# Values products of two query tiles at a time in the dense halves of two attention mixers

## The reference

```python
# first mixer, dense: every query sees all 512 keys
s = (q_nope @ k_nope + q_rope @ k_rope) * scale
o_a = softmax(s) @ v
# first mixer, banded: keys at a distance of at most 128
o_b, lse = banded_attention(qb, kb, vb, 128, 128)
o_b = o_b * sigmoid(lse - sink)
# second mixer: three dilated branches, joined by the softmax of their log sums;
# and attention to a neighbourhood of 8 rows by 16 columns of a 64-column grid, with a bias
o_c = dilated_attention(rope(q_c), rope(k_c), v_c)
o_d = neighborhood_attention(q_d, k_d, v_d, rpb)
```

## Time and profile before

| | |
|---|---|
| median of 3 runs | 2587.31 us |
| profiled execution | 2588.96 us, its span 2586.9 us |
| TensorE (PE) busy | 2502.2 us, 97% |
| DVE, POOL, ACT busy | 1447.5, 723.4 and 553.5 us |
| mean granted clock of TensorE | 0.986 of full speed |
| attention, first mixer | about 132 to 241 us and 349 to 448 us |
| attention, second mixer | about 1383 to 1527 us and 1630 to 1800 us |

### The profile page before, as it was taken

How to read it: one execution, slowest core, us unless ns; L and a number is a source line. 1 busy time by engine, 2 the same in 40 slices (tenths; PEclk the granted TensorE clock), 3 DMA queues, 4 the chain that set the end, 5 groups by cost and what they waited for, 6 DMA issues and landing times. The chain is left out here.

```text
span 2586.9 us, 37035 instructions
## 1 busy us (share of the span) xinstructions
PE 2502.2 (97%) x13964; PEld 1383.0 (53%) x13964; DVE 1447.5 (56%) x2210; ACT 553.5 (21%) x1400; POOL 723.4 (28%) x799
## 2 busy tenths in 40 slices
PE   8999999999999999999899999999989999999997
PEld 4456556445555555555344554454446555565563
DVE  2465456347766866765135332443257767767764
ACT  2164145111111111111103330332111111111112
POOL 2286358123112112120005430542032122121111
PEclk9999999999999999999899999999989999999998
DMA  7100030337999999997600122014249999999986
GB/s 199 27 9 14 1 147 18 116 147 293 330 355 347 341 356 337 345 354 263 214 28 17 54 62 89 17 46 160 98 175 338 345 353 337 345 355 335 354 325 228
DMA packets 177342, 534.91 MB, mean 207 GB/s; under 512 B 32464, under 2 KB 47312, under 8 KB 177232
## 3 DMA queue, kind: packets, MB, share of 16 engines
q1 hardware_dynamic: 166432, 499.34, 51.7%
q0 software_dynamic: 10800, 34.09, 5.8%
HBM read 490.39 MB, written 44.56 MB: 207 GB/s over the span
## 5 line engine op out<-in xcount | busy, mean ns | idle before, releaser
L1857 PE MATMUL bank<-ring,arena 128*64 128x256 f32 x4096 | 479.8, 382 | 2.1 <-DVE arena L2132 1.7
L1868 PE MATMUL bank<-ring,arena 128*128 128x512 f32 x1024 | 453.8, 602 | 1.8 <-ACT arena L1956 1.8
L917 PE MATMUL bank<-ring,arena 128*128 128x512 f32 (+1 forms) x1024 | 430.2, 576 | 1.7 <-issue 0.8
L1857 PEld LDWEIGHTS bank<-ring,arena 128*64 128x64 f32 x4096 | 291.7, 137 | 168.1 <-issue 30.2
L1570 POOL TENSOR_SCALAR arena<-arena 128x512 f32<-128x512 f32 (+2 forms) x256 | 328.0, 1298 | 183.8 <-DVE arena L1446 175.8
L1857 PE MATMUL bank<-arena 128*64 128x256 f32 x3072 | 364.4, 379 | 0.5 <-DVE arena L2001 0.5
L934 PE MATMUL bank<-arena,ring 128*128 128x512 f32 x752 | 328.4, 594 | 4.0 <-DVE arena L1402 4.0
L1868 PEld LDWEIGHTS bank<-ring,arena 128*128 128x128 f32 x1024 | 194.1, 192 | 247.1 <-issue 244.9
L917 PEld LDWEIGHTS bank<-ring,arena 128*128 128x128 f32 x1024 | 193.4, 192 | 208.1 <-issue 201.3
L2188 POOL DMA_INDIRECT residual<-arena x30 | 83.4, 2779 | 776.8 <-DVE arena L2100 776.8
L1857 PEld LDWEIGHTS bank<-arena 128*64 128x64 f32 x3072 | 222.4, 137 | 110.2 <-DVE arena L2001 0.9
(11 more groups left out here) (216 smaller groups left out, 2209.1 us busy)
## 6 DMA issues: line engine op xcount, KB each, us to landing
ring<-in_w_gate SPq DMA_DIRECT2D x64, 2048.0 KB, 9.2
ring<-in_w_up SPq DMA_DIRECT2D x64, 2048.0 KB, 10.4
ring<-in_w_down SPq DMA_DIRECT2D x64, 2048.0 KB, 7.8
ring<-in_w_in_cd SPq DMA_DIRECT2D x6, 2048.0 KB, 16.0
ring<-in_x_in SPq DMA_DIRECT2D x16, 512.0 KB, 4.2
residual<-ring SPq DMA_DIRECT2D x16, 512.0 KB, 2.9
normed<-ring SPq DMA_DIRECT2D x16, 512.0 KB, 2.6
ring<-residual SPq DMA_DIRECT2D x16, 512.0 KB, 5.6
```

The lines of the kernel that those rows point to most:

```text
L917: mm = eng.matmul(bank[banks_of(piece)[k]][0:rows, 0:wide], lhs(c), rhs(c), start=(c == 0), stop=(c == chunks - 1))
L1857: mm = eng.matmul(bank[b][64 * h:64 * h + 64, first_column:first_column + 256], tokens[:, c, :], weights[:, c, 256 * h:256 * h + 256], sta ...
L1868: mm = eng.matmul(bank[6 + b][:, :], lhs[:, 4 * half + c, :], piece[k][:, c, b * BANK:(b + 1) * BANK], start=(half == 0 and c == 0), stop= ...
```

## The change

It has four parts. In the dense halves, `pv` is left out for even tiles; at an odd tile's place it multiplies the values by the transposes of both tiles, 256 columns wide, so that a pair of tiles has 8 products where it had 16. The dense `pT` becomes one buffer for a pair of tiles, laid out by key block with the two tiles side by side, and the copies write strips of 128 columns into it. The banded tiles of the first mixer get a buffer in the ring of weights, which is idle by then. And in the second mixer, `pv` now stands before `turn` in a step; in the first the order stays.

```diff
-                    for v in range(STEPS):
-                        if v + lag(v) == u:
-                            yield "turn", s, STEP[v]
-                    for v in range(STEPS):
-                        if v + lag(v) + 1 == u:
-                            yield "pv", s, STEP[v]
+                    turns = [("turn", s, STEP[v]) for v in range(STEPS) if v + lag(v) == u]
+                    pvs = [("pv", s, STEP[v]) for v in range(STEPS)
+                           if v + lag(v) + 1 == u and not (is_first(STEP[v]) and STEP[v] % 2 == 0)]
+                    yield from (turns + pvs if ab else pvs + turns)
...
+            def pT_of(j, e, s):
+
+                n = width(j)
+                if is_first(j):
+                    o = pT_at + 1024 * e
+                    return arena[:, o:o + 1024].rearrange("p (b t n) -> p b t n", t=2, n=P)[:, :, j % 2, :]
+                if ab:
+                    o = (window_pT0 if s == 0 else 2 * PIECE + 4 * D) + 512 * e
+                    return ring[:, o:o + n]
+                o = pT_at + 512 * (PLACE[j] % 2) + 256 * e
                 return arena[:, o:o + n]
+
+            def pT_pair(e, b):
+
+                o = pT_at + 1024 * e + 2 * P * b
+                return arena[:, o:o + 2 * P]
...
+            def wait_pT_free(eng, s, j):
+
+                if is_first(j):
+                    last = j - 1 if j % 2 == 0 and j else None
+                elif not ab:
+                    last = 15 if j < 18 else before(j, 2)
+                else:
+                    last = before(j, 2)
+                    if j == 16 and s == 0:
+                        eng.wait_ge(pool_s.sem, summed(last_roped(0)))
+                if last is not None:
+                    eng.wait_ge(pe_s.sem, pe_s.after("pv", "pv", s, last))
...
-                                mm = eng.matmul(bank[banks_of(piece)[0]][64 * e:64 * e + 64, t * P:(t + 1) * P], v,
-                                                pT_of(i, e)[:, b * P:(b + 1) * P], start=(b == 0), stop=(b == n_blocks - 1))
+                                if is_first(i):
+                                    columns, turned = slice((t - 1) * P, (t + 1) * P), pT_pair(e, b)
+                                else:
+                                    columns, turned = slice(t * P, (t + 1) * P), pT_of(i, e, s)[:, b * P:(b + 1) * P]
+                                mm = eng.matmul(bank[banks_of(piece)[0]][64 * e:64 * e + 64, columns], v, turned,
+                                                start=(b == 0), stop=(b == n_blocks - 1))
...
-                        if before(i, 2) is not None:
-                            eng.wait_ge(pe_s.sem, pe_s.after("pv", "pv", piece[1], before(i, 2)))
-                        act_s.done(eng.activation(pT_of(i, 0), bank[4][:, 0:width(i)], ACT.Copy), "take0", *piece)
+                        wait_pT_free(eng, piece[1], i)
+                        act_s.done(eng.activation(pT_of(i, 0, piece[1]), turned_of(i, 0), ACT.Copy), "take0", *piece)
```

More of the change, by code:

```diff
@@ L627, in mixer @@
                 rope = wo_region.take(2, SEQ)
+                window_pT0 = wo_region.at
                 tmp = [[wo_region.take(SEQ) for _ in range(2)] for _ in range(2)]
@@ L693, in p_of, with turned_of @@
                 return arena[:, o:o + n]
-            def pT_of(j, e):
-                u, n = PLACE[j], width(j)
-                o = pT_at + (512 * (u % 2) + 256 * e if not ab and j >= 16 else 1024 * (u % 2) + 512 * e)
-                return arena[:, o:o + n]
+            def pT_of(j, e, s):
[7 more added lines that the diff above has]
+                o = pT_at + 512 * (PLACE[j] % 2) + 256 * e
+                return arena[:, o:o + n]
+            def pT_pair(e, b):
+                o = pT_at + 1024 * e + 2 * P * b
+                return arena[:, o:o + 2 * P]
+            def turned_of(j, e):
+                src = bank[4 + e][:, 0:width(j)]
+                return src.rearrange("p (b n) -> p b n", n=P) if is_first(j) else src
+            def wait_pT_free(eng, s, j):
[9 more added lines that the diff above has]
+                    eng.wait_ge(pe_s.sem, pe_s.after("pv", "pv", s, last))
             def p_before(j):
@@ L1125, in pe @@
                         b0 = blocks(i)[0]
-                        if t == 0:
-                            if i % 16 or i and not ab:
-                                wait_taken(eng, ("pv", s, i - 1))
+                        if t == (1 if is_first(i) else 0):
+                            begun = i - t
+                            if begun % 16 or begun and not ab:
+                                wait_taken(eng, ("pv", s, begun - 1))
                             elif ab:
-                                wait_taken(eng, *((("qrturn", T * s + 3), 0) if i == 0 else (("qrv", T * s + 3), 1)))
+                                wait_taken(eng, *((("qrturn", T * s + 3), 0) if begun == 0 else (("qrv", T * s + 3), 1)))
                             else:
@@ L1448, in dve @@
                         eng.wait_ge(pe_s.sem, pe_s.after("turn1", *piece))
-                        if before(i, 2) is not None:
-                            eng.wait_ge(pe_s.sem, pe_s.after("pv", "pv", piece[1], before(i, 2)))
-                        dve_s.done(eng.tensor_copy(pT_of(i, 1), bank[5][:, 0:width(i)]), "take1", *piece)
+                        wait_pT_free(eng, piece[1], i)
+                        dve_s.done(eng.tensor_copy(pT_of(i, 1, piece[1]), turned_of(i, 1)), "take1", *piece)
                     elif what == "pv":
```

## The result

The changed kernel takes 2599.7 us (median of 6 runs, 2598.38 to 2600.24), the kernel before 2587.18 on the same chip (6 runs). The ratio is 1.0046, 95% interval 1.0035 to 1.0056: 12.5 us slower, where 2600 was forecast. Three executions among those that follow took 2940, 5103 and 11339 us and are left out of all fits. Its profiled execution took 2599.35 us with a span of 2597.4, 10.5 more than before.

A forecast was written before the change was run, and what follows sets the result against it. TensorE, busy for 97% of the span, was taken as the bound. First mixer +6.7 and second +6.0 made +12.7 us: 2601.7 from the profiled 2588.96, less 1.65 for the median, so 2600 us; range 2589 to 2607.

The forecast's parts named there:

- The product: Dense tiles, both mixers: a pair takes 1.88 us instead of 2.05, 0.17 saved, 5.4 us over 32 pairs.
- Dense waits of the second mixer: Second mixer, dense part: products wait for ACT's copy, 2.69 us per sequence, +5.4 us for both.
- Steps 8 and 12: Second mixer, dense part: no projection covers ACT's copy before these products, 0.83 us of waiting each.
- Step 16: Second mixer, after short banded scores: product waits 0.83 + 0.43 us, less 0.23 already there, so 1.03.
- Step 4: Second mixer, dense part: copy comes in time, 0; bound of +1.7 us more if this step waits as well.
- Tails of the second mixer: End of the banded part: products directly follow their own transposes, +1.96 us in the first sequence, +1.30 in the second, together +3.3.
- The order elsewhere: Second mixer, rest of banded part: the product waits for the same ACT copy instead of the transposes, 0.
- First mixer: Both sequences: lost cover in half cycles and at the end, product gain included, +6.7 us together.
- The end: First mixer, last dense transposes already wait for ACT; half the pair is paid behind: +0.86 us per sequence, +1.7.
- The cycles: First mixer: eight half cycles with 384-wide scores cost +0.63 us each, +5.0; halves with 256-wide scores 0.
- Rival 3: Clock gives way: two to four new gaps followed by half clock, 1 us each, +2 to 4, about 2603; 6%.
- the second mixer's forecast +6.0: Second mixer in total: 16 pairs save 2.7 us, dense waits cost 5.4, banded ends 3.3.

The follow-up runs named there:

- The experiment with ACT's order: Changed kernel with ACT's copy of transposed probabilities put between the two exponentials in the second mixer's dense steps; 2593.54 us.
- the order alone: Kernel before with only the second mixer's order changed, each product ahead of its step's transposes, products still tile by tile; 2589.58 us.
- the one with the last pair of the first mixer narrow: Kernel before with wide products in the first mixer only, except the last two dense tiles of each sequence, multiplied singly; 2590.22 us.
- the one with the old order in its banded steps: Changed kernel with transposes ahead of products again in the second mixer's banded steps; 2595.10 us.
- the four with the order flipped back: Second mixer's old order restored in the tail: narrow products 2583.61 us; wide, projections moved 2589.89; ACT's copy between exponentials, narrow 2581.84, wide 2581.11.
- the first mixer alone: Kernel before with products two tiles wide, and banded copies in their own buffer, in the first mixer only; 2592.24 us.
- the second mixer alone: Kernel before with only the second mixer changed: products two tiles wide and ahead of transposes; 2593.83 us.
- the filled tail: Changed kernel with unused identity transposes where TensorE waits in the tail of the second mixer's first sequence; 2595.23 us.

## Why the prediction was right, step by step

The forecast of +12.7 met +12.5, with the right sign and by the mechanism that it named, copies that the missing product no longer covers. But two of its terms were wrong in size, a rival held at 6% came true beside it, and that the sum came within 0.2 us is luck.

- *The product.* 1.88 forecast, 1.87 measured, 0.17 a pair. As an estimate by the Trainium skill (TensorE: Matmul & The Clock Gate, Back-to-back issue gap), a pair would take 1.66 at most, 19% under 2.05; the trace does not agree with that for this shape.
- *Dense waits of the second mixer.* Steps 8 and 12: 0.83 forecast, 0.79 and 0.78. Step 16: 1.21, less the 0.23 of before, so 0.98 for 1.03. Step 4: 0 forecast, 0.40; it was named as the upper bound, since the wait of step 3 does not push the copy out of the way. 2.95 a sequence for 2.69, and 5.9 for 5.4. Each stands in both sequences. The experiment with ACT's order shows the mechanism.
- *Tails of the second mixer.* +3.3 forecast; 2.07 + 1.35 = 3.4 in the kernel with the order alone.
- *The order elsewhere.* Here the sum failed: "Elsewhere in the banded part the same ACT copy is waited for, by the product instead of by the transposes: 0." It is a gain of 3.2 +- 0.9 (2.9 by the parts: 0.45 in the dense part of each sequence, 0.85 and 1.20 in the banded part). The first sequence's dense part can't be read by itself, since the clock fell there in that execution; 0.45 is taken over from the second. On balance the waits change little, as forecast: those of 0.20 become some 0.1 shorter ahead of the product, but the one at step 3 grows from 0.83 to 0.93, and steps 16 and 17 wait 0.24 each where step 16 alone waited 0.23. The gain is the projections, 0.19 or 0.20 each once transposes stand in front of them in place of a product; the second sequence has three such in the dense part and six in the banded one, some 1.7 us, and the two parts became 1.65 shorter. The prediction asked only what waits, not what a group costs with another neighbour. The trace of the kernel before had the row: one of its projections stands behind transposes (1722.70, 1723.19, next scores at 1730.16) and shows the 0.49 and the 6.97.
- *First mixer.* +6.7 forecast, +5.4 measured, +5.1 in the trace. The end was right (0.86 and 0.85). The cycles were put at +5.0, 0.63 for each of eight halves with 384-wide scores; +3.4 is left for them. In the second sequence, where the rows of the forecast stood, such a half lost 0.48 (8.50 to 8.98 us from the 384-wide scores to the second dense scores behind them; the first wait is 0.41 for 0.39 forecast) and the other half of the cycle gained 0.09: +0.39 a cycle. In the first sequence the forecast's chain does not hold everywhere: twice the kernel before already waited 0.22 there, the copy comes no earlier, and the whole product turns into waiting, 1.44; such a half lost 0.84 (12.77 to 13.61, as far as the next 256-wide scores). That all this is caused by the missing cover is argued from the timeline; no run took these waits away alone.
- *The clock.* Rival 3 priced two to four places at 1 us each. In the changed kernel one place in the mixers is new, and a dear one: its profiled execution has some 13.6 us at half clock there, which alone lowers the mean clock by 0.0026; over all runs it is 0.9835 for 0.9863, 2.8 times 1.6 us, so 4.5 us. The trace by itself says 5.3: from the last scores to the second group of the next norm's transposes (L989 at 1551.96, L957 at 1540.96) 29.94 us pass, and 24.67 in the kernel with the order alone, whose tail kept its clock. The clock also falls at eight or nine places outside the mixers, in the kernel before as well (at 0.50 from 1254 to 1266, for instance). Rival 3 was not an alternative but an addition.

So +5.1 in the first mixer, +4.4 in the second and 4.5 of clock: 14.0, where 12.5 to 13 was measured (the offsets are known to about 1). Of the second mixer's forecast +6.0, 4.4 is there at equal clock; by the parts of the traces it is less, +1.0 in the second sequence and +1.7 in the first if its tail is put at the 10.00 us of the order alone. The forecast's 12.7 came out because the gain it missed in the order (3) and what it had too much in the first mixer (1.6) nearly cancel the loss it missed in the clock (4.5 to 5.3). At equal clock the change costs 8.6 +- 1.3, two thirds of the forecast.

## What to carry to other kernels

An instruction that is merged or moved leaves a hole, and what the hole uncovers is read from the wait that the same pattern already shows elsewhere: here 0.83 in the one step that had no product. When an order is swapped, price each place where the two neighbours change, gains too, not the one place where it hurts. When a wait was worked out in one stretch, look for the same place in the other sequence before multiplying: two of eight were bound otherwise. And where copies are the limit, put the copy ahead of work that nobody waits for: the order on ACT and the swapped order with its tail spared are worth 4 to 5 us together, the second mixer's wide product under 1.

## What was not expected of the hardware

The clock after a wait is not decided by the wait alone. With a wait of 1.63 to 1.81 us in that tail, the kernel before, the one with the last pair of the first mixer narrow, the one with the old order in its banded steps, the four with the order flipped back and the order alone kept 1.00 in their profiled executions; the first mixer alone, with the old order, fell to 0.50 for about 3.5 us (0.67 from 1522 to 1524, 0.50 from 1524 to 1526); the changed kernel, the second mixer alone and the one with the copy between the exponentials, all with three gaps of 0.61 behind the wait, fell to 0.50 and stayed there for about 10 to 14 us. Another place is the first projection of the second mixer, at about 1377 to 1385: behind a wait of 2.21 us the clock fell to 0.50 in six profiles of seven (not in the kernel before), behind a wait of 1.83, as in the changed kernel, in none of six. Where the clock fell in the tail, the gaps seem to have kept it down, since without them it was back after 3.5 us; that rests on one execution and is not shown. The Trainium skill (TensorE: Matmul & The Clock Gate, What's actually happening) says that "activity releases the throttle"; the filled tail agrees by its mean clock, 0.9857 for 0.9835, and the row of before at 1520 to 1524 does not speak against it, since TensorE was busy there for 2.36 of 4 us. Which executions fall is open: one profile each does not tell how often, only the mean clock of the runs does (0.9847 with the order alone, 0.9863 without).
